# Order of the seven products in split down projections, a weight sum on GpSimd, and four smaller moves in a whole-network kernel

## The reference

```python
def rms_norm(x, g):
    y = x * lax.rsqrt(jnp.mean(x * x, axis=-1, keepdims=True) + EPS)
    return y * g

def swiglu(x, w_gate, w_up, w_down):              # first block, hidden width 2816
    return (jax.nn.silu(x @ w_gate) * (x @ w_up)) @ w_down

def sq_relu_mlp(x, w1, w2):                       # second block, hidden width 4096
    h = jax.nn.relu(x @ w1)
    return (h * h) @ w2

h = h + swiglu(rms_norm(h, norm_ffn), ...)        # then rms_norm(h, norm_final)
...
for layer in range(2):
    m = mixer_a(...) if layer % 2 == 0 else mixer_c(...)
    x = x + rms_norm_2(m, norm_mix_post[layer])
    h = rms_norm_2(x, norm_mlp_pre[layer])
    x = x + rms_norm_2(sq_relu_mlp(h, mlp_w1[layer], mlp_w2[layer]), norm_mlp_post[layer])
```

## Time and profile before

| what | value |
| --- | --- |
| median of three runs | 2062.25 us |
| the profiled execution's own time | 2058.37 us |
| its span in the trace | 2056.6 us |
| TensorE busy | 1959.7 us (95%) |
| DVE busy | 1421.9 us (69%) |
| ACT busy | 947.0 us (46%) |
| GpSimd busy | 31.3 us (2%) |
| mean granted clock | 0.987 |
| weights and activations read | 174.47 MB |

### The profile page before, as it was taken

The page is one execution under the profiler, slowest core; times in us unless marked ns, Lnnn a source line. Parts: engine busy times, 40 slices in busy tenths (PEclk is TensorE's granted clock), DMA queues, the critical chain, the costliest instruction groups (busy, mean ns, idle before and its releaser), DMA issues. The chain is left out here.

```text
span 2056.6 us, 29711 instructions
## 1 busy us (share of the span) xinstructions
PE 1959.7 (95%) x11816; PEld 1068.7 (52%) x11821; DVE 1421.9 (69%) x2460; ACT 947.0 (46%) x1628; POOL 31.3 (2%) x36
## 2 busy tenths in 40 slices
PE   8989999999999999998999999989989999999997
PEld 4444444444444884444445844854544444475475
DVE  4979844548667767677488757868866646985786
ACT  3438733324333334347355434436377844643532
POOL 2000000000000002000000000000000000000000
PEclk9999999999999999999999999999999999999998
DMA  6400233324331333322222531415400031324211
GB/s 219 122 1 1 63 92 103 103 62 133 103 98 43 120 109 119 101 82 62 82 78 72 174 92 58 133 46 156 165 1 1 11 103 41 98 97 159 83 62 42
DMA packets 53930, 179.54 MB, mean 87 GB/s; under 512 B 6176, under 2 KB 11936, under 8 KB 53536
## 3 DMA queue, kind: packets, MB, share of 16 engines
q1 hardware_dynamic: 53792, 177.64, 27.9%
HBM read 174.47 MB, written 2.10 MB: 86 GB/s over the span
## 5 line engine op out<-in xcount | busy, mean ns | idle before, releaser
L2158 DVE SCALAR_TENSOR_TENSOR w_lo<-w_raw,w_hi 128x1024 f16<-128x1024 f32 (+3 forms) x359 | 440.1, 1236 | 72.7 <-ACT w_hi L1711 36.4
L1711 ACT ACTIVATE w_hi<-w_raw 128x1024 f16<-128x1024 f32 (+1 forms) x358 | 373.5, 1063 | 211.6 <-DVE w_raw L2178 88.3
L1149 PE MATMUL pS<-xx,w_hi 128*128 128x512 f16 x952 | 362.9, 381 | 6.6 <-DVE w_lo L2158 3.7
L1150 PE MATMUL pS<-xx,w_hi 128*128 128x512 f16 x952 | 363.0, 381 | 0.0
L1151 PE MATMUL pS<-xx,w_lo 128*128 128x512 f16 x952 | 362.8, 381 | 0.0
L1215 PE MATMUL pS<-arena,w_hi 128*128 128x256 f16 x645 | 177.3, 275 | 13.0 <-issue 7.1
L1216 PE MATMUL pS<-arena,w_hi 128*128 128x256 f16 x645 | 177.4, 275 | 0.0
L1217 PE MATMUL pS<-arena,w_lo 128*128 128x256 f16 x645 | 177.2, 275 | 0.0
L1149 PEld LDWEIGHTS pS<-xx,w_hi 128*128 128x128 f16 x952 | 93.2, 98 | 117.0 <-issue 5.8
L1151 PEld LDWEIGHTS pS<-xx,w_lo 128*128 128x128 f16 x952 | 93.3, 98 | 113.8 <-issue 2.2
L1150 PEld LDWEIGHTS pS<-xx,w_hi 128*128 128x128 f16 x952 | 93.2, 98 | 108.0 <-issue 1.8
(11 more groups left out here) (448 smaller groups left out, 3721.0 us busy)
## 6 DMA issues: line engine op xcount, KB each, us to landing
w_raw<-in_w SPq DMA_DIRECT2D x299, 512.0 KB, 3.8
w_raw<-in_w SPq DMA_DIRECT2D x12, 704.0 KB, 4.0
X<-in_x SPq DMA_DIRECT2D x8, 264.0 KB, 7.1
arena<-in_c SPq DMA_DIRECT2D x2, 1024.0 KB, 7.8
out_t<-X SPq DMA_DIRECT2D x16, 128.0 KB, 1.8
arena<-in_h SPq DMA_DIRECT2D x4, 256.0 KB, 12.4
arena<-in_h SPq DMA_DIRECT2D x2, 512.0 KB, 11.5
arena<-in_c SPq DMA_DIRECT2D x2, 256.0 KB, 2.9
```

Of the source, the lines that this page charges most:

```text
L1149: pe.matmul(ps, wh, ah, start=f, stop=False)
L1150: pe.matmul(ps, wh, al, start=False, stop=False)
L1711: act.activation(to_, from_, ACT.Copy, scale=WS).then_inc(hi_split, 1)
L2158: dve.scalar_tensor_tensor(out=lo_[:, a:], in0=from_[:, a:], scalar=WS, in1=hi_[:, a:], op0=ALU.mult, op1=ALU.subtract).then_inc(lo_split, 1)
```

## The change

1. Product order: S2 comes third and A12 fourth. With the order the banks' waits move too: A12 now follows A11 by two products rather than by one product.
2. Weight sums: GpSimd makes A11 + A21 (S3) from the loaded pieces alone (`add_weights` in its own queue, one for each group, behind the powers of the norms `x1`, `ckv` and `p2`). DVE makes S2 and S1 = S2 - A11 at the point of the first sum, where A11 + A21 now stands in the place of A21: A22 + (A11 + A21) is the old S1, and taking A11 away gives the old S2, so the names of the two change places in the ring (`HELD_IN`, `FREED_BY`). S4 = A12 + the first of them is made apart, at the point of S3. DVE thus makes three sums per group instead of four, 45 instead of 60.
3. The place of loaded A11 is freed by S1 rather than S4, that of A22 by S4 rather than S1.
4. `rhs_ready` for the last pair is waited for ahead of the second product of group 0, no longer ahead of the first. ACT's wait for it in `ffd` goes.
5. `AMONG`: in `x2`, `mb` and `md` DVE takes the second half of the last block from PSUM after 5, 3 and 3 steps of the loop over the first half, no longer behind the loop.
6. `BEHIND`: `dn0a7` and `dn1a7` use bank 4 (`pT`), no longer bank 0.
7. `reach` also lets through units with `after[v]` < 0, the first units of the program.

Cut to its core (names of the sums' counters and the calls of `add_weights` in GpSimd's queue are left out):

```diff
@@ -72,14 +72,15 @@
 INSIDE = {"va": 0, "vb": NQ, "vm": 0, "vv": 0}
+BEHIND = ("dn0a7", "dn1a7")
 UP_A = 16
 B21, B22, B11, B12, T3, T1, T2, T4 = range(8)
-PRODUCTS = (("A11", 0, B11), ("A22", 4, T4), ("A12", 0, B21), ("S2", 1, T2), ("S3", 2, T3), ("S1", 3, T1), ("S4", 5, B22))
+PRODUCTS = (("A11", 0, B11), ("A22", 4, T4), ("S2", 1, T2), ("A12", 0, B21), ("S3", 2, T3), ("S1", 3, T1), ("S4", 5, B22))
 RAWS = ("A21", "A22", "A11", "A12")
-HELD_IN = {"A11": "A11", "A22": "A22", "A12": "A12", "S2": "A11", "S3": "A21", "S1": "A22", "S4": "A12"}
-FREED_BY = {"A21": "S3", "A22": "S1", "A11": "S4", "A12": "S4"}
+HELD_IN = {"A11": "A11", "A22": "A22", "A12": "A12", "S2": "A22", "S3": "A21", "S1": "A11", "S4": "A12"}
+FREED_BY = {"A21": "S3", "A22": "S4", "A11": "S1", "A12": "S4"}
 N_READ = 6
@@ -203,6 +204,8 @@
                     b = 4 + j if j < 2 else turn % 4
+                elif s.name in BEHIND:
+                    b = 4
                 elif s.name in HOME:
@@ -251,8 +254,8 @@
         self.freed += [v[FREED_BY[name]] for name in RAWS]
-        self.sums[v["S2"]] = (raw, v, self.n_sums)
-        self.n_sums += 4
+        self.sums[v["S2"]] = self.sums[v["S3"]] = (raw, v, self.n_sums)
+        self.n_sums += 3
         ends = []
@@ -265,7 +268,7 @@
         s.first_ms.append(ends[0])
-        for x in (2, 3, 3, 5, 5, 6):
+        for x in (3, 3, 3, 5, 5, 6):
             self.out_ms.append(ends[x][0])
@@ -288,7 +291,7 @@
         v = now + 1
-        while v < min(now + 1 + look, stop) and self.after[v] <= now - 2:
+        while v < min(now + 1 + look, stop) and (self.after[v] < 0 or self.after[v] <= now - 2):
             v += 1
@@ -327,6 +330,7 @@
 HALVED = tuple(AHEAD)
+AMONG = {"x2": 5, "mb": 3, "md": 3}
 HT = T // 2
@@ -1069,6 +1075,17 @@
             norm_power("x0", meta=True)
+            def add_weights(name):
+                s = S[name]
+                for g in range(s.n):
+                    raw, _, _ = PL.sums[PL.unit[s.factor(g, 2, 0)]]
+                    for u in (raw["A21"], raw["A11"]):
+                        pool.wait_ge(raw_loaded[u % LOADS], 16 * (u // LOADS + 1))
+                    a, b = w_raw[:, loaded(raw["A21"])], w_raw[:, loaded(raw["A11"])]
+                    pool.tensor_tensor(a, b, a, ALU.add).then_inc(pool_summed, 1)
             filled = [0]
@@ -1198,7 +1220,7 @@
-            def strassen(s, g, ops, copies):
+            def strassen(s, g, ops, copies, r):
@@ -1206,6 +1228,8 @@
                         pe.wait_ge(evicted, free[b] + 1)
+                    if g == 0 and x == 1:
+                        pe.wait_ge(rhs_ready, r)
                     ps = (pS[:, b, 0:HT] if b < 4 else (pT, pO)[b - 4][:, 0, 0:HT])
@@ -1225,9 +1249,8 @@
                     out_pair(parts[0], by_pairs(ops), k, r)
-                pe.wait_ge(rhs_ready, r + parts[0].k)
                 for g in range(parts[1].n):
-                    strassen(parts[1], g, ops, copies)
+                    strassen(parts[1], g, ops, copies, r + parts[0].k)
                 if m is None:
@@ -1700,7 +1723,9 @@
                         act.wait_ge(mm_done, PL.unit_ms[PL.after[v]])
-                    if sum_of(v) is None:
+                    if v in first_sums:
+                        act.wait_ge(pool_summed, first_sums[v] + 1)
+                    elif sum_of(v) is None:
                         act.wait_ge(raw_loaded[u % LOADS], 16 * (u // LOADS + 1))
@@ -2000,7 +2025,6 @@
             act.preload_act_table_set("natural_log_exp_and_others")
-            act.wait_ge(rhs_ready, PL.r["ff"] + KFF1)
             down([S["ffd0"], S["ffds"], S["ffd7"]], 0, 0.5 / WS, "x2")
@@ -2168,16 +2192,16 @@
                 w = {name: w_raw[:, loaded(u)] for name, u in raw.items()}
-                u = raw["A21"]
-                dve.wait_ge(raw_loaded[u % LOADS], 16 * (u // LOADS + 1))
+                if v == units_["S3"]:
+                    dve.wait_ge(summed, first + 1)
+                    dve.wait_ge(lo_split, v)
+                    dve.tensor_tensor(w["A12"], w["A22"], w["A12"], ALU.add).then_inc(summed, 1)
+                    return
+                dve.wait_ge(pool_summed, first // 3 + 1)
                 dve.wait_ge(lo_split, v)
                 dve.tensor_tensor(w["A22"], w["A21"], w["A22"], ALU.add).then_inc(summed, 1)
                 dve.wait_ge(summed, first + 1)
-                dve.tensor_tensor(w["A21"], w["A11"], w["A21"], ALU.add).then_inc(summed, 1)
-                dve.wait_ge(summed, first + 2)
-                dve.tensor_tensor(w["A11"], w["A22"], w["A11"], ALU.add).then_inc(summed, 1)
-                dve.wait_ge(summed, first + 3)
-                dve.tensor_tensor(w["A12"], w["A11"], w["A12"], ALU.add).then_inc(summed, 1)
+                dve.tensor_tensor(w["A11"], w["A22"], w["A11"], ALU.subtract).then_inc(summed, 1)
@@ -2805,14 +2829,14 @@
             for n in range(AHEAD["x2"]):
+                if n == AMONG["x2"]:
+                    ps = out_of(s)
+                    dve.scalar_tensor_tensor(out=X[:, KD - 1, HT:T], in0=ps[:, HT:T], scalar=0.5 / WS, in1=X[:, KD - 1, HT:T],
+                                             op0=ALU.mult, op1=ALU.add).then_inc(evicted, 1)
                 if n == KD - 1:
                     dve.wait_ge(half_taken, i)
                 dve.scalar_tensor_tensor(out=X[:, n, 0:HT], in0=X[:, n, 0:HT], scalar=pcol("g_fin", n), in1=rs[:, 0:HT],
                                          op0=ALU.mult, op1=ALU.mult)
-            ps = out_of(s)
-            dve.scalar_tensor_tensor(out=X[:, KD - 1, HT:T], in0=ps[:, HT:T], scalar=0.5 / WS, in1=X[:, KD - 1, HT:T],
-                                     op0=ALU.mult, op1=ALU.add).then_inc(evicted, 1)
             direct_norm("x2")
@@ -2908,7 +2932,17 @@
                     dve.wait_ge(half_rs, i)
+                    def second_half():
+                        out_of(s, s.n - 1)
+                        if s.n == KD:
+                            dve.wait_ge(squared, PL.q[m] + KD)
+                        taken_to(m, m_view(m, KD - 1)[:, HT:T], out_bank(o)[:, HT:T], 1.0 / WS, s.n < KD).then_inc(evicted, 1)
                     for n in range(ahead + 1):
+                        if s.n < KD and n == AMONG[m]:
+                            second_half()
                         if n < ahead:
@@ -2919,10 +2953,8 @@
                                 ins.then_inc(computed, 1)
-                    out_of(s, s.n - 1)
                     if s.n == KD:
-                        dve.wait_ge(squared, PL.q[m] + KD)
-                    taken_to(m, m_view(m, KD - 1)[:, HT:T], out_bank(o)[:, HT:T], 1.0 / WS, s.n < KD).then_inc(evicted, 1)
+                        second_half()
                     dve.wait_ge(half_taken, i)
```

More of the change, by code:

```diff
@@ L1048, in loaded @@
             return slice(PL.raw_at[u] * P, (PL.raw_at[u] + PL.raw_size[u]) * P)
[L1050 removed]
+        place_of = {"S2": 0, "S1": 1, "S4": 2}
+        first_sums = {v["S3"]: n for n, (_, v, _) in enumerate(x for u, x in PL.sums.items() if u == x[1]["S2"])}
         sum_index = {v[name]: first + x for _, v, first in PL.sums.values() for name, x in place_of.items()}
```

7 lines of the change are left out of this document (6 added, 1 removed).

## The result

The changed kernel takes 2046.44 us (median of four runs, 2044.77 to 2047.94) against 2061.85 for the kernel before (four runs): ratio 0.9924, with an interval of 0.9907 to 0.9941. It is 15.4 us faster; 21.5 were forecast, and the range of 2032 to 2051 held the time. The profiled execution took 2046.04 us with a span of 2044.2, 12.3 less than the profiled one before.

What follows compares the result with a forecast made beforehand. TensorE, busy 1959.7 of 2056.6 us, bounds the kernel; only its 97 us of standing still and its clock can give. Gains of 24.45 less 3 for GpSimd make 21.5: 2062.25 to 2040.7, rounded to 2040.5, range 2032 to 2051.

Steps and rivals of the forecast that it cites:

- The start: First units, rest of unit 1 let through sooner by `reach`: TensorE's waits and half clock go, 9.1 us, lower bound 3.
- the bank of `dn0a7` and `dn1a7`: Last output blocks of dn0a and dn1a: two waits at L2751 go with the other bank, gain 1.9 us.
- the last halves: x2, mb, md: earlier PSUM read shortens waits for the last square, 1.2, 2.8 and 2.0 us, sum 6.0, bounds 3 and 7.6.
- the reading of the "issue" waits as bank 0's: Four group entries, 7.1 us: TensorE waits for DVE's read of bank 0, not for tokens; gain 2.5 from one sum less.
- the moved token wait: Group entries: waiting later for the last pair's `rhs_ready` is worth nothing; a rival (0.06) gave it nearly all of 7.1 us.
- the half clock: Start, behind the 6.69 us stop: TensorE's clock granted at 0.50, 3.4 us of work at half speed, worth 1.7 us.
- The waits for the copy in `dn0b` and `dn1b`: Four TensorE waits for ACT's copy of A11: S2 ahead of A12 gives 2.61 us more, so 2.85 us go.
- Sums on GpSimd: Sums moved from DVE may slow DVE beside them: cost 0 to 7.1 us, 3 taken.
- the 5.1: Cost in us of GpSimd's sums beside DVE by the two Trainium skill pages, which would make the gain 19.4.
- Block 1: Group 1 of `ffd`: chain from loaded A11 to ACT's copy leaves 1.1 of a 3.22 us gap, gain 2.1, bounds 0 and 3.2.
- The one with the full price: Rival, chance 0.28: GpSimd and DVE shut each other out, 7.1 us off 24.45, gain 17.3, time 2045.0.
- the rule of the Trainium skill: SBUF page: a DVE instruction with two SBUF inputs and a GpSimd SBUF operation each wait for the whole of the other.

Runs made afterwards that it cites:

- both bank runs: First output blocks of dn0a, dn0b, dn1a, dn1b in bank 5, not bank 0: on the changed kernel 2033.81 us, on the kernel before 2051.73.

## Why the prediction was right in sum and wrong in one step

**Right.** The start, by its cause (9.1 forecast, 8.4 measured alone, no stop behind the one of 0.93 at 7.99), the bank of `dn0a7` and `dn1a7` (1.9 and 1.9, in the profile only), the last halves (6.0 and 6.6), the reading of the "issue" waits as bank 0's (both bank runs), and with it that the moved token wait is worth nothing.

**Right in sum by luck.** Two terms of the start were misread, and the errors cancel. The prediction let the half clock end at about 23.7 us and priced it at 1.7. In the trace of before it goes on to 25.0:

```profile
24.00:25.00 1.00, 1.00 (x3) 0.30 (x2) 1.00 (x4) 0.00 (x0) 0.00 (x0) 0.50 0.94 191
25.00:26.00 1.00, 1.00 (x6) 0.50 (x5) 1.00 (x8) 0.00 (x0) 0.00 (x0) 0.95 1.00 365
```

Matmuls start 0.42 us apart from 20.39 to 25.03 rather than 0.21, which costs 2.3. And the second wait at 25.3, priced at 0.7, is not there: TensorE is busy for the whole of both windows. The wait of 6.7 and these 2.3 make 9.0, by chance the 9.1 of the forecast.

**Right size, wrong cause.** The waits for the copy in `dn0b` and `dn1b`: 2.85 forecast from the 2.61 us that S2 puts between. They went with the old order as well and stayed with the new one when DVE kept the sum. The step took the new order as the gain, and counted the missing sum at the entries alone.

**Wrong.** The step "Sums on GpSimd", priced at 3 with an upper end of 7.1. It took "its whole length falls on DVE in the queue ahead of an entry" once for each entry, but GpSimd works as soon as the pieces land, and those of group 0 and of group 1 both land while DVE is behind: 2 x 2.2 us at `dn0a` and 2 x 1.6 at `dn1a`. Against that the sum that DVE is spared, 1.23, is small. And it left out that TensorE's clock can fall behind such stops, which cost 1.7 us at each of the two entries in this profile. The 2.45 and 2.2 of its upper end, and the 5.1, stand in the prediction without their working. So `dn0a` and `dn1a` came out at +4.8 and +3.6 where -0.7 each stood in the sum before the 3 were taken off: 9.8 us against 3. These 6.8 are the whole miss of 6.1 and more.

**Block 1.** 2.1 forecast, 0.5 measured. The chain was right in its first link: the piece is loaded some 9 us later relative to the products, as worked out. The rest of S2 came 2.2 us behind the forecast, 1.7 of it from the `w_lo` that GpSimd's sum held (3.30 us instead of 1.62).

**The rivals.** The one with the full price, 2045.0, is what happened by its cause, and the rule of the Trainium skill by which it was given is the one that the rows confirm. That its time came within 1.5 us of 2046.44 is in part luck: its 7.1 was too little for the same miscount (9.8), as was the 5.1, and two executions of the kernel before differ by 4.2. The trace of before had no row in which a GpSimd instruction that reads SBUF met DVE, so the mean of the two ends was a choice, and the rule was the only thing that told them apart.

What stays open: why the stop ahead of L1386 in the second mixer is 1.55 us in one execution of the same program and 2.79 in another, and why TensorE's clock falls behind a stop in some executions and not in others. Between two executions of the kernel before this made 4.2 us, more than most single terms here.
